# Two gate products inside a slab chunk, and a slab ahead of the transposes, in the rounds of layer 0

## The chip, the cores and the metric

The kernel runs on one core of a Trainium2 chip. The metric is the time on the device in microseconds. A core has TensorE (PE in the rows; PEld are its weight loads), VectorE (DVE), ScalarE (ACT), GpSimd (POOL) and SyncE (SP), whose queue starts all the DMA transfers here. The engines run side by side; each works through its own instructions in order and waits on semaphores for the others.

## The reference, cut to what matters

A two-layer backbone on 1024 latent tokens and 256 context tokens (1280 in all) with 1024 features. Only layer 0 is touched by the change. With h the normed and modulated input:

```python
z = h @ w_in                         # 1024 -> u, g, f, gf, 1024 columns each
u = centred_depthwise_conv(u, w_conv, b_conv)      # 4 taps
for d in range(2):                                 # both directions
    r = sigmoid(block_diag_linear(u, w_a[d], b_a[d]))
    i = sigmoid(block_diag_linear(u, w_x[d], b_x[d]))
    log_a = -8 * r * softplus(-lam[d])
    a = exp(log_a)
    b = sqrt(-expm1(2 * log_a)) * (i * u)
    y += linear_scan(a, b)                         # over tokens
f = fft2(f grouped by 128 channels, axes=(tokens, channels)).real
mix = concatenate([y * silu(g), (f @ w_f + b_f) * silu(gf)])
out = mix @ w_out
```

Matrix products are computed to nearly float32 precision: each operand is split into a high and a low part, and three products (high by high, high by low, low by high) are summed. The kernel calls such a triple mm3.

## The kernel before, in words

Layer 0 begins with a setup (norm, modulation), which makes `h_hi` and `h_lo`, eight blocks of 128 features by 1280 tokens. Then come eight rounds, t = 0 to 7, each for 128 channels. The first and the last are written out, the six between are a loop. The text counts them as rounds one to eight. A round multiplies four slabs of 128 columns of `w_in` by h, named SLAB_U, SLAB_F, SLAB_GF and SLAB_G (in the text U, F, GF, G). Tokens fall into three chunks of 512, 512 and 256 (`CHUNKS`). All the four slab products go to the same three PSUM banks `slab`, one for each chunk, so a bank must be read before the next slab writes it. The other products (gates, transposes, DFT, its second stage UV) share the PSUM buffer `W`, and `W4`.

Order of TensorE in a round before (`body`, L854): U, F (in round one both are made beside the setup, U in `slab` and F in `W`), transposes of f (L866), two small products with w_f (L874), six gate products of direction 0, GF, six gate products of direction 1, the DFT (30 products), G, and UV. A gate product k writes bank k mod 4 of `W`, and from k = 4 on it waits on `gr` for the tanh that read that bank. Product k = 6d + 3x + c belongs to direction d, gate x and chunk c.

Order of ScalarE: w_hi of F, u from PSUM, first tap of the convolution (L535), w_hi of GF, gate weights `gw_hi`, `u_hi` (L543), f from PSUM (L548), in round one the tanh of the two rows of conditions (L557), the transposed f from PSUM (L560), `ab_hi`, then for direction 0 the six tanh of the gates (L498) and three functions of the whole (L505, L507, L511), w_hi of G (L482), `y_hi` (L568, it shares the tile pq_hi), the square root (L516), tanh of GF (L574), and direction 1 in the same way; `pq_hi` (L577) comes after the DFT.

Order of VectorE: convolution taps, products with the modulation weights (`mod_sums`, L610, which use the tile E as ScalarE's L505 does), butterflies of the DFT, then for direction 0 the product i*u (L683), the term under the root (L686), b (L691), two scans (L697, L700), after these `sgf` (L711, three pieces, which read the slab banks of GF and count up `sgfd`), direction 1, `pq_lo` (L717), the scan backwards (L704), the gate of G (L721, three pieces, which count up `sg`), and the output. GpSimd makes the low parts: `w_lo` (L759), `gw_lo`, `u_lo` (L769), `y_lo` (L772). SP loads slabs of weights into `wraw` in one order for all (`body`, L430). SLAB_G's product waits for `sgfd`, SLAB_U's for `sg`.

After layer 0 come its output projection (L1183), layer 1's projections (L1453), attention and the last projection (L2016), which the change doesn't touch.

Of the kernel before, what the change touches and what calls it, by code (L numbers as in the profile page):

```python
# [23 lines left out]
ACT = mybir.ActivationFunctionType  # L24
# [3 lines left out]
KT = D // P  # L28
# [5 lines left out]
CHUNKS = [(0, 512), (512, 512), (1024, 256)]  # L34
# [311 lines left out]
def mixers(nc, a, h_hi, h_lo, work, cols, silu_c, gs, ident, mods, wraw, w_hi, w_lo, slab, W, W4, before):  # L346
    ctx = ExitStack()
    with ctx:
# [8 lines left out]
        u_hi, u_lo = sb("u_hi", [P, T], F32R), sb("u_lo", [P, T], F32R)  # L357
        cur = sb("cur", [P, ALL_COLS])
        gw = sb("gw", [P, 4, P])
        gw_hi, gw_lo = sb("gw_hi", [P, 4, P], F32R), sb("gw_lo", [P, 4, P], F32R)  # L360
        A, B, C, H, sgf, fT, xf, u = (work[:, i, :] for i in range(KT))
# [50 lines left out]
        @blk.sync  # L412
        def _(sp):
            def load_slab(t, j, first):
                if not (first and j < 2):
                    sp.wait_ge(wl[j % 2], 2 * t + j // 2)
                sp.dma_start(wraw[:, j % 2, :], a["w_in0"][4 * t + j]).then_inc(w_ld[j % 2], 16)

            def store(t):
                sp.wait_ge(mr, t + 1)  # L420
                sp.dma_start(a["mixT"][t], H[:]).then_inc(mrs, 16)
                sp.wait_ge(mf, t + 1)
                sp.dma_start(a["mixT"][t + KT], xf[:]).then_inc(mfs, 16)

            def load_mod(t, q, first):
                if not (first and q < 2):
                    sp.wait_ge(mp, 2 * (N_MOD * t + q - 1))
                sp.dma_start(wm1[:, q % 2, :], a["wm1"][t, q]).then_inc(m_ld[q % 2], 16)

            def body(t, first, last):  # L430
                if first:
                    load_mod(t, 0, True)
                    load_mod(t, 1, True)
                    sp.wait_ge(zero, 2)
                else:
                    sp.wait_ge(gwl, t)
                for c in range(2):
                    sp.dma_start(gw[HEAD * c:HEAD * (c + 1), :, HEAD * c:HEAD * (c + 1)],
                                 a["w_gate"][t, HEAD * c:HEAD * (c + 1), :, :]).then_inc(gw_ld, 16)
                if not first:  # L440
                    sp.wait_ge(abp, t)
                sp.dma_start(wf[:], a["w_f"][t]).then_inc(wf_ld, 16)
                load_slab(t, SLAB_GF, first)
                load_slab(t, SLAB_G, first)
                if not first:
                    store(t - 1)
                load_mod(t, 2, first)
                if not last:
                    load_slab(t + 1, SLAB_U, False)
                load_mod(t, 3, first)  # L450
                if not last:
                    load_slab(t + 1, SLAB_F, False)
                    load_mod(t + 1, 0, False)
                    load_mod(t + 1, 1, False)

            set_sync(sp, lambda j: load_slab(0, j, True))
            sp.wait_ge(hl, 4)
            for raw, at in tab_pieces:
                sp.dma_start(raw, a["tables"][:, at]).then_inc(tab_ld, 16)
            sp.wait_ge(modk, KT)  # L460
            sp.dma_start(silu_b[:], a["c_rows"].partition_broadcast(P)).then_inc(cb_ld, 16)
            sp.dma_start(dft_ch[:], a["dft_ch"]).then_inc(par, 16)
            loops(sp, body)
            store(KT - 1)
            sp.wait_ge(ge, 2)
            for i in range(2):
                sp.dma_start(a["gp"][i].rearrange("w (k n) -> (w k) n", n=P), g_rows[:, i, :]).then_inc(gst, 16)
            sp.wait_ge(mrs, 16 * KT)
            sp.wait_ge(mfs, 16 * KT)
            sp.wait_ge(gst, 32)  # L470
# [3 lines left out]
        def _(act):  # L474
            def split_hi(t, j, first=False):

                act.wait_ge(w_ld[j % 2], 16 * (2 * t + j // 2 + 1))
                if j >= 2:
                    act.wait_ge(done[j - 2], 3 * t + 3)
                elif not first:  # L480
                    act.wait_ge(done[j + 2], 3 * t)
                nc.scalar.activation(w_hi[:, j % 2].rearrange("p k n -> p (k n)"), wraw[:, j % 2, :],  # L482
                                     ACT.Copy).then_inc(wh[j % 2], 1)
# [30 lines left out]
            def root(t, d):  # L514
                act.wait_ge(om, 2 * t + d + 1)
                nc.scalar.activation(C[:], C[:], ACT.Sqrt).then_inc(sq, 1)  # L516

            def body(t, first, last):
                if not first:
                    split_hi(t, SLAB_F)  # L520
# [12 lines left out]
                if not first:  # L533
                    act.wait_ge(mp, 2 * N_MOD * t + 2)
                nc.scalar.activation(E[:], u_raw[:, 0:CONV_N], ACT.Identity, scale=cur[:, C_CONV:C_CONV + 1],  # L535
                                     bias=cur[:, C_BCONV:C_BCONV + 1]).then_inc(tap0, 1)
                split_hi(t, SLAB_GF)
                act.wait_ge(gw_ld, 32 * t + 32)
                if not first:
                    act.wait_ge(gp_, 12 * t)  # L540
# [2 lines left out]
                nc.scalar.activation(u_hi[:], u[:], ACT.Copy).then_inc(uh, 1)  # L543
                if not first:
                    act.wait_ge(yd, t)
                for c, (at, n) in enumerate(CHUNKS):
                    act.wait_ge(s_f, 3 * t + c + 1)
                    nc.scalar.activation(fT[:, at:at + n], (W if first else slab)[:, c, 0:n], ACT.Copy).then_inc(fr, 1)  # L548
                if not first:
                    act.wait_ge(mfs, 16 * t)  # L550
                if first:
                    act.wait_ge(cb_ld, 16)
                    act.wait_ge(conv, 2)
                    for w in range(2):
                        if w:
                            act.wait_ge(sbd, 1)
                        nc.scalar.activation(E[:, 0:D], silu_b[:, w, :], ACT.Tanh, scale=0.5).then_inc(thb, 1)  # L557
                for c, (at, n) in enumerate(CHUNKS):
                    act.wait_ge(trd, 3 * t + c + 1)
                    nc.scalar.activation(xf[:, at:at + n], W[:, c, 0:n], ACT.Copy).then_inc(xr, 1)  # L560
                act.wait_ge(abp, t + 1)
                nc.scalar.activation(ab_hi[:], W4[:, 0:256], ACT.Copy).then_inc(abh, 1)
                gates(t, 0, first)
# [220 lines left out]
        def _(pe):  # L784
            def mm3(out, l_hi, l_lo, r_hi, r_lo, start, stop):
                nc.tensor.matmul(out, l_hi, r_hi, start=start, stop=False)  # L786
                nc.tensor.matmul(out, l_hi, r_lo, start=False, stop=False)  # L787
                return nc.tensor.matmul(out, l_lo, r_hi, start=False, stop=stop)  # L788
# [9 lines left out]
                        if k == KT - 1:  # L798
                            last.then_inc(done[j], 1)

            def slab_product(t, j, first):
                pe.wait_ge(wl[j % 2], 2 * t + j // 2 + 1)
                for c, (at, n) in enumerate(CHUNKS):

                    if j == SLAB_F:
                        pe.wait_ge(ur, 3 * t + c + 1)
                    elif j == SLAB_GF:
                        pe.wait_ge(fr, 3 * t + c + 1)
                    elif j == SLAB_G:
                        pe.wait_ge(sgfd, 3 * t + c + 1)  # L810
                    elif not first:
                        pe.wait_ge(sg, 3 * (t - 1) + c + 1)
                    for k in range(KT):
                        last = mm3(slab[:, c, 0:n], w_hi[:, j % 2, k, :], w_lo[:, j % 2, k, :],
                                   h_hi[:, k, at:at + n], h_lo[:, k, at:at + n], k == 0, k == KT - 1)
                    last.then_inc(done[j], 1)

            def gate_products(t, d):
                for x in range(2):
                    for c, (at, n) in enumerate(CHUNKS):  # L820
                        k = 6 * d + 3 * x + c
                        if k < 3:
                            pe.wait_ge(xr, 3 * t + k + 1)
                        elif k > 3:
                            pe.wait_ge(gr, 12 * t + k - 3)
                        mm3(W[:, k % 4, 0:n], gw_hi[:, 2 * d + x, :], gw_lo[:, 2 * d + x, :],
                            u_hi[:, at:at + n], u_lo[:, at:at + n], True, True).then_inc(gp_, 1)

            def dft_product(t):
                pe.wait_ge(gr, 12 * t + 12)  # L830
# [23 lines left out]
            def body(t, first, last_):  # L854
                if first:
                    set_tensor(pe, first_products)
                else:
                    slab_product(t, SLAB_U, first)
                    slab_product(t, SLAB_F, first)
                pe.wait_ge(fr, 3 * t + 3)  # L860
                if first:
                    pe.wait_ge(par, 16)
# [10 lines left out]
                for x in range(2):  # L873
                    last = nc.tensor.matmul(W4[:, x * P:(x + 1) * P], dft_ch[:, x * P:(x + 1) * P], wf[:],  # L874
                                            start=True, stop=True)
                last.then_inc(abp, 1)
                pe.wait_ge(gwl, t + 1)
                pe.wait_ge(ul, t + 1)
                gate_products(t, 0)
                slab_product(t, SLAB_GF, first)  # L880
                gate_products(t, 1)
                dft_product(t)
                slab_product(t, SLAB_G, first)
                pe.wait_ge(pql, t + 1)
                pe.wait_ge(abl, t + 1)

# [1271 lines left out]
```

## Time and profile before

| | us |
|---|---|
| median of 3 runs | 1574.29 |
| lowest, highest | 1569.56, 1576.51 |
| profiled execution, span from first to last instruction | 1569.5 |
| TensorE busy (share of the span) | 1405.4 (90%) |
| VectorE busy | 856.1 (55%) |
| ScalarE busy | 729.8 (46%) |
| GpSimd busy | 572.1 (36%) |
| mean granted TensorE clock | 0.955 |

The profiled execution's time is its span, which is as long as the lowest of the runs. A busy engine's share is a mean over stages; the first 90 us are the setup, layer 0's rounds last until about 680 us, and the rest is the output projection and layer 1. TensorE's clock has two levels, 2.4 GHz (1.00 in the rows) and 1.2 GHz (0.50).

### The profile page before, as it was taken

What the parts mean: (1) busy time and instruction counts of PE and PEld (TensorE: products, weight loads), DVE (VectorE), ACT (ScalarE), POOL (GpSimd) and SP (SyncE); (2) the same over time, 40 slices, a digit from 0 to 9 for tenths busy, and PEclk for the clock granted to TensorE, in tenths of its full rate; (3) what the DMA queues carried; (4) which work ended last, traced back from release to release, by engine and by line L of the source; (5) the groups of instructions that cost most, each with busy time, mean ns of one, the idle gap of its engine ahead of it and who ended that gap; (6) DMA issues with size and microseconds to landing.
All of it is one profiled execution on the core that took longest, in us unless ns stands there. A gap on an engine that the chain in (4) does not pass through costs nothing. (4 is left out here: it accounts for less than half of the span.)

```text
span 1569.5 us, 19994 instructions
## 1 busy us (share of the span) xinstructions
PE 1405.4 (90%) x7136; PEld 1161.0 (74%) x7136; DVE 856.1 (55%) x1216; ACT 729.8 (46%) x1146; POOL 572.1 (36%) x267
## 2 busy tenths in 40 slices
PE   4968999999999999938999985999996999998697
PEld 2557888888888888836888864878885788887576
DVE  4577768677758686743111125122221888887532
ACT  3356364554656373733122213132221888887321
POOL 0013222331313323235244323434442666665432
PEclk7978999999999999969999996999998999999799
DMA  9131212122121212055433416634335533222674
GB/s 378 33 125 60 88 59 87 63 101 86 67 92 53 101 49 90 12 175 209 126 102 111 130 65 219 161 94 127 101 108 144 200 94 89 91 83 68 187 220 129
DMA packets 95284, 179.61 MB, mean 114 GB/s; under 512 B 10464, under 2 KB 57344, under 8 KB 92928
## 3 DMA queue, kind: packets, MB, share of 16 engines
q1 hardware_dynamic: 95232, 178.93, 35.4%
q8 instruction: 31, 0.51, 0.1%
q14 instruction: 21, 0.17, 0.0%
HBM read 123.84 MB, written 45.11 MB: 108 GB/s over the span
## 5 line engine op out<-in xcount | busy, mean ns | idle before, releaser
L786 PE MATMUL slab<-h_hi,w_hi 128*128 128x512 f32 x744 | 265.9, 357 | 0.1
L788 PE MATMUL slab<-h_hi,w_lo 128*128 128x512 f32 x744 | 265.3, 357 | 0.0
L787 PE MATMUL slab<-h_lo,w_hi 128*128 128x512 f32 x744 | 265.2, 356 | 0.0
L759 POOL TENSOR_TENSOR w_lo<-wraw,w_hi 128x1024 fp32r<-128x1024 f32 x32 | 81.6, 2551 | 421.6 <-ACT w_hi L482 421.6
L1738 POOL TENSOR_TENSOR probs<-probs,rdenom 128x2560 f32<-128x2560 f32 (+1 forms) x32 | 135.7, 4242 | 57.9 <-DVE rdenom L1698 57.9
L786 PEld LDWEIGHTS slab<-h_hi,w_hi 128*128 128x128 f32 x744 | 139.6, 188 | 23.2 <-DVE h_lo L259 0.3
L787 PEld LDWEIGHTS slab<-h_lo,w_hi 128*128 128x128 f32 x744 | 139.6, 188 | 22.7
L788 PEld LDWEIGHTS slab<-h_hi,w_lo 128*128 128x128 f32 x744 | 139.6, 188 | 22.7
L1453 PE MATMUL slab<-h_hi,w_hi 128*128 128x512 f32 (+1 forms) x352 | 135.5, 385 | 18.0 <-DVE h_lo L1375 18.0
L1183 PE MATMUL Y<-wo_hi,m_hi 128*128 128x512 f32 x320 | 127.6, 399 | 23.6 <-DVE wo_lo L1098 19.6
L1454 PE MATMUL slab<-h_lo,w_hi 128*128 128x512 f32 (+1 forms) x352 | 134.9, 383 | 0.0
L1455 PE MATMUL slab<-h_hi,w_lo 128*128 128x512 f32 (+1 forms) x352 | 134.6, 382 | 0.0
L1184 PE MATMUL Y<-wo_lo,m_hi 128*128 128x512 f32 x320 | 125.8, 393 | 0.0
L1185 PE MATMUL Y<-wo_hi,m_lo 128*128 128x512 f32 x320 | 125.6, 393 | 0.0
L1715 DVE TENSOR_TENSOR pt_lo<-TB,pt_hi 128x512 fp32r<-128x512 f32 x152 | 104.1, 685 | 33.7 <-ACT pt_hi L1661 32.0
L1635 ACT ACTIVATE probs<-probs,neg_max 128x640 f32<-128x640 f32 (+1 forms) x128 | 102.7, 803 | 24.9 <-DVE neg_max L1690 24.4
L1690 DVE CUSTOM_DVE_ANT_0 probs<-S,mask,nsink 128x640 f32<-128x640 f32 (+1 forms) x128 | 107.5, 842 | 1.5 <-PE S L1765 1.3
L1764 PE MATMUL S<-kd_hi,q_parts 128*128 128x256 f32 (+2 forms) x256 | 88.2, 349 | 13.9 <-DMA q_parts<-qT 12.5
L610 DVE SCALAR_TENSOR_TENSOR E<-wm,silu_bcast 128x1024 f32<-128x1024 f32 x64 | 97.6, 1525 | 5.5 <-DMA wm<-in_wm 1.1
L1661 ACT ACTIVATE pt_hi<-TB 128x512 fp32r<-128x512 f32 x152 | 89.5, 589 | 22.1 <-PE TB L1799 22.1
L1799 PE MATMUL TB<-ident,probs 128*128 128x128 f32 x608 | 91.0, 272 | 1.5 <-POOL probs L1738 1.5
L1799 PEld LDWEIGHTS TB<-ident,probs 128*128 128x128 f32 x608 | 75.6, 140 | 22.2 <-issue 1.7
(257 smaller groups left out, 3010.8 us busy)
## 6 DMA issues: line engine op xcount, KB each, us to landing
wraw<-in_w_in SPq DMA_DIRECT2D x32, 512.0 KB, 3.6
wm<-in_wm SPq DMA_DIRECT2D x32, 512.0 KB, 3.4
mixT<-work SPq DMA_DIRECT2D x16, 640.0 KB, 4.0
mraw<-mixT SPq DMA_DIRECT2D x20, 512.0 KB, 4.7
wm<-in_wm SPq DMA_DIRECT2D x8, 1024.0 KB, 20.4
q_parts<-qT SPq DMA_DIRECT2D x32, 256.0 KB, 4.6
oT<-o_out SPq DMA_DIRECT2D x8, 1024.0 KB, 3.9
work<-in_xT SPq DMA_DIRECT2D x8, 640.0 KB, 11.7
```

The source lines that it names most:

```text
L786: nc.tensor.matmul(out, l_hi, r_hi, start=start, stop=False)
L787: nc.tensor.matmul(out, l_hi, r_lo, start=False, stop=False)
L788: return nc.tensor.matmul(out, l_lo, r_hi, start=False, stop=stop)
L1183: nc.tensor.matmul(out, m_hi[:, s, h, k, :], w_hi, start=(h == 0 and k == 0), stop=False)
L1184: nc.tensor.matmul(out, m_hi[:, s, h, k, :], w_lo, start=False, stop=False)
L1185: last = nc.tensor.matmul(out, m_lo[:, s, h, k, :], w_hi, start=False, stop=(h == 1 and k == KT - 1))
L1453: nc.tensor.matmul(out, w_hi[:, j, k, :], rhs_hi, start=(k == 0), stop=False)
L1454: nc.tensor.matmul(out, w_hi[:, j, k, :], rhs_lo, start=False, stop=False)
L1455: last = nc.tensor.matmul(out, w_lo[:, j, k, :], rhs_hi, start=False, stop=(k == KT - 1))
L1690: nc.vector.tensor_tensor_reduce(out=row(b, pr[:, u, h, :]), in0=S[:, j % 2, at:768], in1=m, scale=-SCALE, scalar=nsink[:, j:j + 1], op0=A ...
L1738: nc.gpsimd.tensor_tensor(rows, rows, rden[:, u, :].unsqueeze(2).to_broadcast(rows.shape), ALU.mult).then_inc(pn, 1)
L1799: last = nc.tensor.transpose(TB[:, n_par(b, u, x), h * P:(h + 1) * P], pr[:, u, h, x * P:(x + 1) * P], ident[:])
```

## The change

On TensorE a slab product can now be issued by chunks, and a chunk by halves (`slab_chunk` with k0 and k1), and the gate products by a range.

- All rounds: gate products 4 and 5 of direction 0 stand behind the first half (k = 0 to 3, 12 products) of a GF chunk (chunk 0, in round one chunk 2). Gate products 10 and 11 stand behind the first half of G's chunk 0, and its second half comes ahead of the DFT. G's chunks 1 and 2 stay behind the DFT.
- Round one: chunk 0 of GF is issued ahead of the transposes, chunk 1 behind the products with w_f. Chunk 0 of GF waits for `ur` in place of `fr`. ScalarE copies f and the transposed f (`f_rows`, `f_tokens`) right behind w_hi of GF, ahead of gw_hi, u_hi and the condition rows. SP loads GF and G right behind the tables.

```diff
@@ SP, body and ahead of it
-                load_slab(t, SLAB_GF, first)
-                load_slab(t, SLAB_G, first)
-                if not first:
+                if not first:
+                    load_slab(t, SLAB_GF, first)
+                    load_slab(t, SLAB_G, first)
                     store(t - 1)
...
                 sp.dma_start(raw, a["tables"][:, at]).then_inc(tab_ld, 16)
+            load_slab(0, SLAB_GF, True)
+            load_slab(0, SLAB_G, True)
             sp.wait_ge(modk, KT)
@@ ScalarE
+            def f_rows(t, first):
+                for c, (at, n) in enumerate(CHUNKS):
+                    act.wait_ge(s_f, 3 * t + c + 1)
+                    nc.scalar.activation(fT[:, at:at + n], (W if first else slab)[:, c, 0:n], ACT.Copy).then_inc(fr, 1)
+
+            def f_tokens(t):
+                for c, (at, n) in enumerate(CHUNKS):
+                    act.wait_ge(trd, 3 * t + c + 1)
+                    nc.scalar.activation(xf[:, at:at + n], W[:, c, 0:n], ACT.Copy).then_inc(xr, 1)
...
                 split_hi(t, SLAB_GF)
+                if first:
+                    act.wait_ge(hl, 2 * KT)
+                    f_rows(t, first)
+                    f_tokens(t)
                 act.wait_ge(gw_ld, 32 * t + 32)
...
                 if not first:
                     act.wait_ge(yd, t)
-                for c, (at, n) in enumerate(CHUNKS):
-                    act.wait_ge(s_f, 3 * t + c + 1)
-                    nc.scalar.activation(fT[:, at:at + n], (W if first else slab)[:, c, 0:n], ACT.Copy).then_inc(fr, 1)
-                if not first:
+                    f_rows(t, first)
                     act.wait_ge(mfs, 16 * t)
+                    f_tokens(t)
...
-                for c, (at, n) in enumerate(CHUNKS):
-                    act.wait_ge(trd, 3 * t + c + 1)
-                    nc.scalar.activation(xf[:, at:at + n], W[:, c, 0:n], ACT.Copy).then_inc(xr, 1)
                 act.wait_ge(abp, t + 1)
@@ TensorE
+            def slab_chunk(t, j, c, first, k0=0, k1=KT):
+                at, n = CHUNKS[c]
+                if k0 == 0:
+                    if c == 0:
+                        pe.wait_ge(wl[j % 2], 2 * t + j // 2 + 1)
                     if j == SLAB_F:
                         pe.wait_ge(ur, 3 * t + c + 1)
                     elif j == SLAB_GF:
-                        pe.wait_ge(fr, 3 * t + c + 1)
+                        pe.wait_ge(ur if first else fr, 3 * t + c + 1)
                     elif j == SLAB_G:
                         pe.wait_ge(sgfd, 3 * t + c + 1)
...
+                for k in range(k0, k1):
+                    last = mm3(slab[:, c, 0:n], w_hi[:, j % 2, k, :], w_lo[:, j % 2, k, :],
+                               h_hi[:, k, at:at + n], h_lo[:, k, at:at + n], k == 0, k == KT - 1)
+                if k1 == KT:
                     last.then_inc(done[j], 1)
...
+                if first:
+                    slab_chunk(t, SLAB_GF, 0, first)
                 pe.wait_ge(fr, 3 * t + 3)
...
                 last.then_inc(abp, 1)
+                if first:
+                    slab_chunk(t, SLAB_GF, 1, first)
                 pe.wait_ge(gwl, t + 1)
                 pe.wait_ge(ul, t + 1)
-                gate_products(t, 0)
-                slab_product(t, SLAB_GF, first)
-                gate_products(t, 1)
+                gate_products(t, 0, range(0, 4))
+                slab_chunk(t, SLAB_GF, 2 if first else 0, first, 0, 4)
+                gate_products(t, 0, range(4, 6))
+                slab_chunk(t, SLAB_GF, 2 if first else 0, first, 4, KT)
+                if not first:
+                    slab_chunk(t, SLAB_GF, 1, first)
+                    slab_chunk(t, SLAB_GF, 2, first)
+                gate_products(t, 1, range(0, 4))
+                slab_chunk(t, SLAB_G, 0, first, 0, 4)
+                gate_products(t, 1, range(4, 6))
+                slab_chunk(t, SLAB_G, 0, first, 4, KT)
                 dft_product(t)
-                slab_product(t, SLAB_G, first)
+                slab_chunk(t, SLAB_G, 1, first)
+                slab_chunk(t, SLAB_G, 2, first)
```

## Rows read from the trace of the kernel before

**Rows 1.** The page: its span, and GpSimd's low part of a slab.

```profile
span 1569.5 us, 19994 instructions
...
L759 POOL TENSOR_TENSOR w_lo<-wraw,w_hi 128x1024 fp32r<-128x1024 f32 x32 | 81.6, 2551 | 421.6 <-ACT w_hi L482 421.6
```

**Rows 2.** One period (A:B, length, busy by engine, PEclk), and TensorE's wait in it.

```profile
234.20:307.40 73.20, 71.36 (x382) 60.46 (x381) 53.08 (x63) 40.99 (x50) 21.38 (x8) 1.00 0.23 78
...
PE W L786 <- ACT work L498: 1.4, 2, 1.1
```

**Rows 3.** TensorE in order of time (start, length), round two.

```profile
191.12 0.48 PE L786 MATMUL W<-u_hi,gw_hi 128*128 128x512 f32 x1
...
194.72 0.39 PE L786 MATMUL slab<-h_hi,w_hi 128*128 128x512 f32 x1
...
208.72 0.39 PE L786 MATMUL W<-u_hi,gw_hi 128*128 128x512 f32 x1
...
214.04 0.39 PE L786 MATMUL W<-tab_hi,pq_hi 128*128 128x256 f32 x1 [1.15 <-ACT work L498]
...
217.67 0.39 PE L786 MATMUL slab<-h_hi,w_hi 128*128 128x512 f32 x1
...
234.14 0.40 PE L786 MATMUL slab<-h_hi,w_hi 128*128 128x512 f32 x1
```

**Rows 4.** ScalarE and VectorE in order of time, round two, and a window of it.

```profile
192.10 3.52 ACT L498 ACTIVATE work<-W,cur 128x512 f32<-128x512 f32 x6
...
195.50:204.50 9.00, 9.00 (x40) 7.23 (x39) 5.25 (x13) 8.93 (x8) 3.68 (x2) 1.00 0.01 4
...
204.53 2.99 DVE L691 SCALAR_TENSOR_TENSOR work<-work 128x1280 f32<-128x1280 f32 x1 [3.70 <-ACT work L516]
...
210.64 1.59 DVE L711 SCALAR_TENSOR_TENSOR work<-work,slab 128x512 f32<-128x512 f32 x3
...
218.07 1.65 ACT L577 ACTIVATE pq_hi<-W 128x1792 fp32r<-128x1792 f32 x1
...
228.38 0.69 DVE L721 SCALAR_TENSOR_TENSOR work<-work,slab 128x512 f32<-128x512 f32 x1 [0.67 <-ACT work L584]
```

**Rows 5.** Round one: order of time on three engines, and a window.

```profile
92.52 1.46 ACT L535 ACTIVATE E<-u_raw,cur 128x1282 f32<-128x1282 f32 x1
...
97.00:103.50 6.50, 0.00 (x0) 0.00 (x0) 3.91 (x3) 4.09 (x6) 5.05 (x3) 0.50 0.08 31
...
103.52 1.28 ACT L557 ACT_TABLE_LOAD   x1
...
103.55 0.48 PE L866 MATMUL W<-ident,work 128*128 128x128 f32 x1 [11.15 <-ACT work L548]
...
118.30 1.46 ACT L505 ACTIVATE E<-work,cur 128x1280 f32<-128x1280 f32 x1 [3.42 <-DVE E L610]
...
135.41 1.59 DVE L711 SCALAR_TENSOR_TENSOR work<-work,slab 128x512 f32<-128x512 f32 x3
```

**Rows 6.** Four waits of TensorE after layer 0, each with the window behind it.

```profile
713.16 0.77 PE L1183 MATMUL Y<-wo_hi,m_hi 128*128 128x512 f32 x1 [2.28 <-POOL wo_lo L1151]
...
713.10:716.50 3.40, 3.34 (x8) 2.69 (x9) 2.13 (x2) 1.16 (x2) 2.12 (x1) 0.51 0.69 228
...
724.84 0.50 PE L1183 MATMUL Y<-wo_hi,m_hi 128*128 128x512 f32 x1 [3.06 <-DVE wo_lo L1098]
...
724.80:728.20 3.40, 2.53 (x10) 1.79 (x11) 2.08 (x1) 2.96 (x4) 3.32 (x2) 1.00 0.99 388
...
969.18 0.77 PE L1453 MATMUL slab<-h_hi,w_hi 128*128 128x512 f32 x1 [3.21 <-DVE h_lo L1375]
...
969.10:972.40 3.30, 3.21 (x8) 2.58 (x9) 3.24 (x1) 0.39 (x1) 2.16 (x1) 0.50 0.00 0
...
1479.55 0.50 PE L2016 MATMUL Y<-wo_hi,m_hi 128*128 128x512 f32 x1 [2.43 <-POOL m_lo L1983]
...
1481.00:1484.40 3.40, 3.40 (x9) 2.67 (x9) 3.37 (x3) 0.00 (x0) 2.74 (x1) 0.50 0.00 0
```

More of the change, by code:

```diff
@@ L799, in first_products @@
                             last.then_inc(done[j], 1)
-            def slab_product(t, j, first):
-                pe.wait_ge(wl[j % 2], 2 * t + j // 2 + 1)
-                for c, (at, n) in enumerate(CHUNKS):
+            def slab_chunk(t, j, c, first, k0=0, k1=KT):
[3 more added lines that the diff above has]
+                        pe.wait_ge(wl[j % 2], 2 * t + j // 2 + 1)
                     if j == SLAB_F:
@@ L812, in slab_product, with gate_products @@
                         pe.wait_ge(sg, 3 * (t - 1) + c + 1)
-                    for k in range(KT):
-                        last = mm3(slab[:, c, 0:n], w_hi[:, j % 2, k, :], w_lo[:, j % 2, k, :],
-                                   h_hi[:, k, at:at + n], h_lo[:, k, at:at + n], k == 0, k == KT - 1)
+                for k in range(k0, k1):
+                    last = mm3(slab[:, c, 0:n], w_hi[:, j % 2, k, :], w_lo[:, j % 2, k, :],
+                               h_hi[:, k, at:at + n], h_lo[:, k, at:at + n], k == 0, k == KT - 1)
+                if k1 == KT:
                     last.then_inc(done[j], 1)
[L818 to L827, printed above, removed]
+            def slab_product(t, j, first):
+                for c in range(3):
+                    slab_chunk(t, j, c, first)
+            def gate_products(t, d, ks):
+                for k in ks:
+                    x, c = k // 3, k % 3
+                    at, n = CHUNKS[c]
+                    k += 6 * d
+                    if k < 3:
+                        pe.wait_ge(xr, 3 * t + k + 1)
+                    elif k > 3:
+                        pe.wait_ge(gr, 12 * t + k - 3)
+                    mm3(W[:, k % 4, 0:n], gw_hi[:, 2 * d + x, :], gw_lo[:, 2 * d + x, :],
+                        u_hi[:, at:at + n], u_lo[:, at:at + n], True, True).then_inc(gp_, 1)
             def dft_product(t):
```

## The prediction

> **What bounds the kernel now.** I read the share of busy time first, then the waits of TensorE, and then one round in order of time. The profiled execution spans 1569.5 us, and the three timed runs go from 1569.56 to 1576.51, so next to nothing lies around the span; the sum below is made against 1569.5, and carried over to the median of 1574.29, which is 4.8 above it [rows 1]. Rounds two to eight of layer 0 repeat to a hundredth of a microsecond with a period of 73.2 us. TensorE is busy for 71.4 of it at full clock, and waits 1.4 us for ScalarE's tanh of the gate products [rows 2]. So a round is bound by TensorE, but a second chain runs just beside it: gate products of direction 0, tanh (L498), three exponentials, two splits, root, b-term, scan. ScalarE has no gap in the middle of that chain (8.9 busy of 9.0 us) [rows 4]. VectorE begins to empty the first slab bank (L711) at 210.64, while TensorE gets through its four free gate products of direction 1 at 211.2 (208.72 plus 3.5 units of 0.70) [rows 3, 4]. The two chains meet within half a microsecond, and what makes the second longer will soon be seen.
>
> Durations: from 194.72 to 208.72 one slab of 48 products of 512 columns and 24 of 256 takes 14.00 us, so 0.233 us per 512 columns, 2.80 for half a chunk, 5.60 for a chunk, 0.70 or 0.35 for a gate product [rows 3].
>
> **Rounds two to eight, step by step.**
> 1. Direction 0. Gate products 0 to 3 take 2.45 us from 191.12, as before. Then 2.80 us of slab GF go ahead of products 4 and 5. Before, ScalarE's six tanh ended at 195.62 (192.10 plus 3.52) [rows 3, 4]. Product 4 now starts at 196.46 and product 5 ends its turn at 197.51; with the lag of 0.9 us that the rows show from there to the end of the sixth tanh (194.72 to 195.62), it ends near 198.4: 2.78 later. ScalarE works in order and without a gap behind it, so exponentials, w_hi of slab G, y_hi and root move by 2.78. TensorE gains nothing here, since it had no wait at products 4 and 5: the 18 products took 3.60 of the ideal 3.50 [rows 3]. The cover that was given away is that of ScalarE's chain.
> 2. The b-term is 2.99 us long at 204.53, because GpSimd's y_lo runs into it; y_lo comes from the same ScalarE chain and moves with it, so this keeps its length. The Trainium skill ("SBUF — State Buffer", "The single rule") calls this an exclusive lock between the two engines, which agrees with that row. L711's three pieces (512, 512, 256 columns in 1.59 us) begin at 213.42 and the first ends at 214.1 [rows 4].
> 3. The new first half of slab G's chunk 0 writes the bank that this piece reads: it waits for sgfd. TensorE is through with products 6 to 9 at 211.2 and waits until 214.2, about 3 us. Queued behind the waiting product are the last two gate products, the rest of chunk 0, the DFT. Before, TensorE came to slab G only after the DFT, and sgfd was long there.
> 4. From 214.2: 2.80 of slab, 1.05 of gate products 10 and 11, 2.80 of slab, so the DFT starts at 220.85 instead of 214.04. The wait for the last tanh is really gone: their tanh end near 218.9, by the same lag of 0.9.
> 5. From the DFT's start two ways lead to the next round. TensorE: before, 20.10 us to 234.14; now one chunk less, 14.50: 235.35. The other: DFT 3.63, then pq_hi (218.07 before, 0.4 behind the DFT, of which the exponentials made 0.2), and 11.00 us from there to the end of the first L721 piece (228.38 plus 0.69), whose read frees the bank for the next slab U. I take 3.63 + 0.2 + 11.0 + 0.1 = 14.95: 235.8 [rows 3, 4]. The later one counts: **+1.67 us per round**, for six rounds 10.0. The eighth has no next slab U and splits one slab less; there the TensorE way counts, +1.2.
>
> One term hangs on how fast the products follow each other. The trace has 233 ns for 512 columns [rows 3]. The Trainium skill ("TensorE: Matmul & The Clock Gate", "Wait — 56ns, not 53.3ns?") gives N over 2.4 GHz plus some 2.5 ns, 216 ns for 512 columns. By the Trainium skill's figure the three half chunks that are new on the path would be 0.6 us shorter, and the round +1.0 instead of +1.67. The row is of these very products, so the sum keeps it.
>
> **Clock.** A stall of 3 us is new. The trace has four of about that length: after those of 2.28, 2.43 and 3.21 us a stretch of 3.4 us follows at 0.5 of the clock (1.2 GHz), after one of 3.06 us none [rows 6]. In such a stretch eight 512-column products run in 3.4 us instead of fourteen and a half: 1.55 us lost, all of it on the path. Three in four over seven rounds: **+8.1**, bounds 0 and 10.9; twice the upper one if the clock needs two such stretches to come back.
>
> **Round one.** Loads of slabs GF and G go behind the tables, where SP's queue is idle; they are the same two DMAs, moved ahead of silu rows, channel DFT, two wm1 pieces, gate weights and W_f, all of which wait for modk, so that they are issued no later than before. ScalarE is done with the first tap at 93.98 and makes w_hi, some 1 us, without waiting for a transfer, GpSimd w_lo takes 2.55, and chunk 0 of GF starts at 97.6 instead of the transposes at 103.55 [rows 1, 5]. With some 4 us of it at half clock it ends near 105.2, so the transposes come 1.7 later than before. ScalarE waits for them in front of gw_hi and u_hi. Of its 4.1 us of work in 97.0 to 103.5 (w_hi, gw_hi, u_hi, three copies of equal size to those of the transposes) all but w_hi's 1 us now follows the first transposed bank (106.0, an estimate: 0.8 behind the first transpose), so its next piece, the table load for the tanh of the condition rows, moves from 103.52 to 109.3: +5.8. Behind that table load stand silu rows, VectorE's six mod_sums, and the exponential at 118.30, which waited 3.4 us for exactly these [rows 5]. So the whole chain moves by 5.8, and L711's first piece ends at 135.41 + 0.69 + 5.8 = 141.9. Chunk GF0 fills half of TensorE's 11.15 us gap, but the work done early only makes TensorE wait at G's chunk 0: the transposes, W_f and GF1 last to 112.5, the gate products of direction 0 with GF2 to 119.0, four more gate products to 121.5, and there TensorE stands until 142. Then 10.3 us to the DFT's end, plus 2.0 for half clock: 154.4; plus 0.2 + 11.0 + 0.1: slab U at 165.8, against 160.94 before (234.14 less a period). **+4.9**; the bounds I take are 3 and 7 (no half clock at all, or twice as long).
>
> Sum: 4.9 + 10.0 + 1.2 + 8.1 = **24.2 us**. The profiled execution becomes 1593.7, the median 1598.5. Behind layer 0 nothing changes.
>
> **Rivals.** 0.5% of this kernel, about what a measurement can tell from no change, is 7.9 us.
> - *No half clock.* As above, but the stall doesn't bring the clock down. For it: one of four stalls didn't; against it: the three that did. 16.1 us, 1590.4.
> - *Long half clock.* Each stall is followed by two stretches at 0.5: 7 times 3.1 in place of 8.1, +38, 1612. For it: round one's gap of 11 us kept the clock at 0.5 to its end [rows 5]; against it: after three shorter stalls it was 3.4 us each time [rows 6].
> - *Round one gives its gap back.* If the mod_sums chain weren't put off by the transposes, the 11.15 us of idle would be won, and the rounds' loss of 19 remains: +8, 1582. Against it: ScalarE's order of instructions.
> - *The other side: ScalarE's chain has slack.* The point is the delay of the last tanh. At 2.78 us a round gets 1.67 longer; it is one for one, so below 1.1 us of delay the round gets shorter. With none, TensorE reaches slab G at 211.4, the next U comes at 233.0, -1.1 a round, and round one -1.2: -9, 1565. Against it: 8.9 busy of 9.0 us on ScalarE [rows 4].
>
> **Numbers.** Forecast 0.56; no half clock 0.20; long half clock 0.07; round one gives back 0.07, half of it below +7.9; other side 0.06, small mixtures near nothing 0.04. So faster by over 0.5% 0.06, within 0.5% 0.08, slower 0.86. The range goes from 1584, which leaves out the last two cases and part of the third rival, to 1610. Predicted: 1598.5.
>
> **What the changed profile would show.** Per round TensorE waits some 3 us at the first slab product behind gate product 9, released by VectorE L711's line, and none at the DFT; period near 76; half-clock stretches near most of those waits. In round one no long wait before the transposes, but one of about 20 us before slab G. It would be wrong if the period stayed under 73.2: then the sixth tanh wasn't on the chain; or if ScalarE's table load in round one came before 106.

## The result, and the profile after

The changed kernel takes 1596.37 us (median of 4 runs, 1593.73 to 1601.22), the kernel before 1573.67 in the same comparison (1569.56 to 1576.51). The ratio is 1.0157, with a 95% interval of 1.0135 to 1.0178: some 25 us slower (21 to 28); the two medians themselves lie 22.7 apart. The profiled execution spans 1596.2 us, within a timed execution of 1597.96.

Both traces hold a mark that the setup and layer 1 don't touch: from ScalarE's first copy of u out of PSUM (91.12 before, 92.40 after) to the last products of layer 0, the two transposes of `mods` (679.7 before). Between them lie the eight rounds and nothing else. Below, "in layer 0" means this stretch, in the one profiled execution of a kernel: 588.6 us before. It has a spread of its own, in round one: in the traces of seven kernels here whose round one has the same instructions, the kernel before among them, slab U of round two starts between 68.6 and 70.7 us behind the first copy of u. So of a difference in layer 0, up to 2 us can be chance; the six periods behind repeat to 0.2 us where the clock is full.

The page of the changed kernel, its head and its group of slab products (line 797 is the first product of mm3, line 722 is L711 of before, line 732 is L721):

```profile
span 1596.2 us, 19995 instructions
...
L797 PE MATMUL slab<-h_hi,w_hi 128*128 128x512 f32 x744 | 272.7, 367 | 48.4 <-DVE work L722 40.8
```

The two transposes at the end of layer 0 in the view of instructions by tile (least, median and most ns of one, then the start of the first and of the last):

```profile
L929 PE MATMUL W<-ident,mods x2: 380/398/417, 706.1 to 706.3; 128*16 128x128 f32 x2
```

706.1 less 92.40 is 613.7 us in layer 0: +25.1. The slab products, which waited for nothing before, now wait 40.8 us for VectorE's reading of the slab banks. The waits for the tanh [rows 2] are gone from the list, and so is the one of 11 us ahead of round one's transposes [rows 5]:

The waits of TensorE in the whole of the changed kernel (sum, count, longest):

```profile
PE slab L797 <- DVE work L722: 40.8, 8, 20.7
...
PE slab L797 <- POOL w_lo L770: 5.4, 1, 5.4
...
PE W L886 <- ACT work L523: 3.3, 7, 0.5
PE slab L797 <- DVE work L732: 2.1, 7, 0.4
```

Round four of the changed kernel, which ran at full clock, in order of time on TensorE: slab U, slab G's chunk 0, the DFT, the rest of slab G, the next slab U. It answers to [rows 3].

```profile
321.11 0.50 PE L797 MATMUL slab<-h_hi,w_hi 128*128 128x512 f32 x1 [0.30 <-DVE work L732]
...
374.50 0.47 PE L797 MATMUL slab<-h_hi,w_hi 128*128 128x512 f32 x1 [2.88 <-DVE work L722]
...
381.22 0.28 PE L797 MATMUL W<-tab_hi,pq_hi 128*128 128x256 f32 x1
...
384.73 0.40 PE L797 MATMUL slab<-h_hi,w_hi 128*128 128x512 f32 x1
...
396.01 0.50 PE L797 MATMUL slab<-h_hi,w_hi 128*128 128x512 f32 x1 [0.30 <-DVE work L732]
```

The same round as a window: its length, the busy time of TensorE, its weight loads, VectorE, ScalarE and GpSimd, the granted clock, the DMA share and GB/s:

```profile
321.11:396.01 74.90, 71.25 (x380) 60.26 (x380) 53.18 (x64) 40.80 (x51) 21.35 (x9) 1.00 0.22 76
```

The period is 74.90 where it was 73.20. From slab U to the DFT (the product at 381.22) it is 60.11 us (53.10 before), and from the DFT to the next slab U 14.79 (20.10 before).

ScalarE at the same place of round two, to be held beside [rows 4]: four tanh, a gap for the half chunk, the last two, and the exponential.

```profile
198.26 2.45 ACT L500 ACTIVATE work<-W,cur 128x512 f32<-128x512 f32 x4
203.52 1.05 ACT L500 ACTIVATE work<-W,cur 128x512 f32<-128x512 f32 x2 [2.81 <-PE W L799]
204.47 1.46 ACT L507 ACTIVATE E<-work,cur 128x1280 f32<-128x1280 f32 x1
```

The 7 us behind each of the seven waits of 2.8 to 2.9 us; the last column but two is the granted clock:

```profile
220.40:227.40 7.00, 7.00 (x20) 5.57 (x21) 0.77 (x2) 2.06 (x5) 0.00 (x0) 0.57 0.02 4
298.00:305.00 7.00, 6.96 (x25) 5.63 (x26) 1.37 (x3) 3.27 (x7) 0.00 (x0) 0.76 0.00 0
374.50:381.50 7.00, 7.00 (x33) 5.77 (x34) 2.27 (x3) 4.84 (x8) 0.00 (x0) 1.00 0.00 0
449.40:456.40 7.00, 7.00 (x33) 5.77 (x34) 2.25 (x3) 4.82 (x8) 0.00 (x0) 1.00 0.00 0
524.30:531.30 7.00, 7.00 (x20) 5.61 (x21) 0.76 (x2) 2.11 (x5) 0.00 (x0) 0.57 0.00 0
601.90:608.90 7.00, 7.00 (x25) 5.67 (x26) 1.37 (x3) 3.27 (x7) 0.00 (x0) 0.76 0.00 0
678.30:685.30 7.00, 7.00 (x33) 5.77 (x34) 2.24 (x3) 4.75 (x7) 0.00 (x0) 1.00 0.01 2
```

Four waits have low clock (1.2 GHz) behind them, two for nearly all of the 7 us and two for about half; three have none. The reader sees it in the number of products: 20, 25 or 33 in the same time. Slab U starts at 167.03, 244.68, 321.11, 396.01, 470.90, 548.53 and 625.04, so the six periods are 77.65, 76.43, 74.90, 74.89, 77.63 and 76.51. Twice 74.9 stands where the clock was full, some 2.7 more where it was low for long, some 1.6 more where for half of that.

Round one of the changed kernel, beside [rows 5]:

```profile
99.09 0.79 PE L797 MATMUL slab<-h_hi,w_hi 128*128 128x512 f32 x1 [5.42 <-POOL w_lo L770]
...
110.53 1.28 ACT L571 ACT_TABLE_LOAD   x1
...
125.86 1.45 ACT L507 ACTIVATE E<-work,cur 128x1280 f32<-128x1280 f32 x1 [6.05 <-DVE E L621]
...
143.63 0.76 PE L797 MATMUL slab<-h_hi,w_hi 128*128 128x512 f32 x1 [20.70 <-DVE work L722]
...
167.03 0.50 PE L797 MATMUL slab<-h_hi,w_hi 128*128 128x512 f32 x1 [0.20 <-DVE work L732]
```

This trace reached ScalarE's first copy of u 1.28 us later than that of before, so from each of these times 1.28 is taken: the table load stands at 109.25 (103.52 before), the exponential at 124.58 (118.30), slab U of round two at 165.75 (160.94).

So the +25.1 us in layer 0 are: round one +4.8; six periods, 458.0 against 439.0 (before they are 73.12 to 73.20 us each), +19.0; the last round and what follows it +1.3. Of the 19.0, 10.4 is the longer period at full clock (six times 74.90 less 439.0), and 8.6 the low clock. This split is that of one execution; in the others the low clock may have had another share, since the mean clock was 0.953 in the quickest of the four and 0.947 in the slowest.

### The profile page after: what moved, and what is told of

It is laid out like the page before. It is cut to its first block and busy times, and to the rows that moved or that the text cites. A ratio compares the mean times of both kernels' runs of the same rounds, so it can differ in the third digit from the quotient of the medians.

```text
span 1596.2 us, 19995 instructions
## 1 busy us (share of the span) xinstructions
PE 1415.2 (89%) x7136; PEld 1167.6 (73%) x7136; DVE 855.3 (54%) x1216; ACT 727.7 (46%) x1146; POOL 571.6 (36%) x267
## 5 line engine op out<-in xcount | busy, mean ns | idle before, releaser
L797 PE MATMUL slab<-h_hi,w_hi 128*128 128x512 f32 x744 | 272.7, 367 | 48.4 <-DVE work L722 40.8
L798 PE MATMUL slab<-h_lo,w_hi 128*128 128x512 f32 x744 | 269.8, 363 | 0.0
L799 PE MATMUL slab<-h_hi,w_lo 128*128 128x512 f32 x744 | 269.4, 362 | 0.0
L798 PEld LDWEIGHTS slab<-h_lo,w_hi 128*128 128x128 f32 x744 | 142.8, 192 | 22.7
L1484 PE MATMUL slab<-h_hi,w_hi 128*128 128x512 f32 (+1 forms) x352 | 135.4, 385 | 18.7 <-DVE h_lo L1406 18.1
## 6 DMA issues: line engine op xcount, KB each, us to landing
work<-in_xT SPq DMA_DIRECT2D x8, 640.0 KB, 12.4
```

Of the source, the lines that this page charges most:

```text
L1484: nc.tensor.matmul(out, w_hi[:, j, k, :], rhs_hi, start=(k == 0), stop=False)
```

## The experiments

Theory: two chains run side by side; the split in direction 0 makes ScalarE's longer, slab G's chunk 0 meets the bank that VectorE reads only behind the scan, and the low clock comes on top; in round one the place of ScalarE's copy puts off the condition rows. The rivals are in the expectations. Each kernel was timed beside the kernel before. The ratio stands with its 95% interval, and beside it the change in layer 0, which is free of what varies outside that layer.

**One part alone.** Round one only; direction 0 only; direction 1 only (the last two with round one as before):

```diff
 # round one only: rounds two to eight as before
-                gate_products(t, 0, range(0, 4))
...
+                gate_products(t, 0, range(0, 6))
+                slab_chunk(t, SLAB_GF, 0, first, 0, KT)
...
+                gate_products(t, 1, range(0, 6))
+                dft_product(t)
+                slab_chunk(t, SLAB_G, 0, first, 0, KT)
...
 # direction 0 only
                 gate_products(t, 0, range(0, 4))
                 slab_chunk(t, SLAB_GF, 0, first, 0, 4)
                 gate_products(t, 0, range(4, 6))
...
+                gate_products(t, 1, range(0, 6))
+                dft_product(t)
+                slab_chunk(t, SLAB_G, 0, first, 0, KT)
...
 # direction 1 only
+                gate_products(t, 0, range(0, 6))
+                slab_chunk(t, SLAB_GF, 0, first, 0, KT)
...
                 gate_products(t, 1, range(0, 4))
                 slab_chunk(t, SLAB_G, 0, first, 0, 4)
                 gate_products(t, 1, range(4, 6))
                 slab_chunk(t, SLAB_G, 0, first, 4, KT)
                 dft_product(t)
```

> Only round one is changed (slab GF ahead of the transposes, the new order of ScalarE and SP, its own gate products and slab G as in the changed kernel); rounds two to eight are those of before. Theory (ScalarE's wait for the transposes puts off the condition rows, the mod_sums and with them the scan): +4.9 us, TensorE waits some 20 us at slab G of round one, and the period stays 73.2. Rival (the 11 us gap ahead of the transposes is won): -8 to -11 us. Rival (round one has no part in it): 0.

Measured: ratio 1.0041 (1.0026 to 1.0056), +6 us; in layer 0 +6.2. TensorE's wait at slab G of round one is 20.67 us, and the periods behind stay at 73.16 to 73.24. The gap of 11 us that the slab fills is not won, and round one is worse for it.

> Only gate products 4 and 5 of direction 0 stand behind half of GF's chunk 0, in rounds two to eight; direction 1, slab G and round one are as before. Theory (the last tanh of direction 0 is at the head of the chain to the scan, and its delay goes through one for one): the scan ends 2.8 us later, TensorE waits 3 us for the tanh of gate product 6, the period at full clock is 76.0 (+2.8), and half-clock stretches come on top: +19.5 and some 8, so +24 to +30 us. Rival (ScalarE's chain has slack): 0 to +3 us.

Measured: ratio 1.0243 (1.0229 to 1.0257), +38 us; in layer 0 +37.0. The direction is the theory's, the amount is above its range. In the trace the wait is the forecast one. It stands at gate product 10, since the tanh of direction 1 that has to free its bank starts only behind the scan. What was wrong is the clock:

```profile
215.82 0.50 PE L792 MATMUL W<-u_hi,gw_hi 128*128 128x512 f32 x1 [3.00 <-ACT work L498]
218.28 0.58 PE L792 MATMUL W<-tab_hi,pq_hi 128*128 128x256 f32 x1 [0.69 <-ACT work L498]
```

The first line is the wait ahead of gate product 10, the second the one behind it, ahead of the transform. The windows behind three of the seven waits:

```profile
215.80:222.80 7.00, 6.29 (x27) 5.80 (x28) 3.82 (x5) 6.57 (x8) 0.00 (x0) 0.55 0.01 4
294.00:301.00 7.00, 6.03 (x27) 5.60 (x28) 3.82 (x5) 6.58 (x8) 0.00 (x0) 0.57 0.00 0
...
450.80:457.80 7.00, 5.86 (x27) 5.51 (x28) 3.83 (x5) 6.50 (x8) 0.00 (x0) 0.58 0.00 0
```

All seven waits have a clock between 0.55 and 0.61 in the 7 us behind them, where I had counted on three in four at half the length.

> Only direction 1: gate products 10 and 11 stand inside slab G's chunk 0, which comes ahead of the DFT, in rounds two to eight; direction 0 and round one are as before. Theory: the bank is free at 211.4 when TensorE comes at 211.2, so the wait at slab G is 0.2 us instead of 2.9, the DFT starts 4.1 later but the two waits of 1.4 us are filled, the period is 72.1 (-1.1, set by the chain behind the DFT), no half clock in rounds two to eight: -8 us. Rival (slab G ahead of the DFT is itself what costs, since pq, root and the second scan start later): +1 to +4 us a round, +7 to +28.

Measured: ratio 0.9952 (0.9938 to 0.9966), -8 us; in layer 0 -7.7. The period is 72.1 (slab U at 233.41, 305.51 and 377.61), no wait stands ahead of slab G, and 0.30 us at slab U. So direction 1's part gains 8 us alone, and slab G ahead of the DFT costs nothing by itself. Direction 0's part costs 37 alone, and it turns the whole into a loss.

**The clock alone.** The time in which TensorE would wait is filled with products that nobody reads, in the changed kernel and in the one with direction 0 alone (there ahead of gate product 10).

```diff
                 gate_products(t, 1, range(0, 4))
+                if not first:
+                    pe.wait_ge(abl, t + 1)
+                    for i in range(24):
+                        nc.tensor.matmul(W4[:, 256:512], u_hi[:, 0:P], h_hi[:, 0, 0:256], start=True, stop=True)
                 slab_chunk(t, SLAB_G, 0, first, 0, 4)
```

> The changed kernel, and in rounds two to eight TensorE makes 24 products of 256 columns, whose result nobody reads, in the time in which it would wait for slab G's bank (2.8 of 2.9 us). Theory (the stall's half clock costs some 8 us of the change's 23, and the rest is the longer chain): all rounds at 1.00 of the clock, period 74.9 everywhere, +15 to +17 us against before. Rival (the clock has no part, the work is late for another reason): as the changed kernel, +23 us, or more for the added products.

Measured: ratio 1.0108 (1.0091 to 1.0126), +17 us; in layer 0 +16.8 against +25.1 of the changed kernel. The period is 74.87 to 74.97, also in the rounds where the clock had been low, and from 150 to 660 us all is at 1.00:

```profile
168.06:242.93 74.87, 74.10 (x405) 63.25 (x405) 53.20 (x64) 40.81 (x51) 21.36 (x9) 1.00 0.23 77
```

24 more products in each of rounds two to eight, and the kernel is 8 us faster. The low clock is 8.3 us of the change's 25.

> The kernel with the split in direction 0 alone, with 24 products of 256 columns (2.8 us) that nobody reads ahead of gate product 10 in rounds two to eight. Theory (its +37 us are 7 times 2.8 for the chain and 7 times 2.5 for half clock): the clock stays at 1.00, the period is 76.0, +19 to +21 us against before. Rival (the chain got longer by more than the split): 78 us a round, +34 to +38.

Measured: ratio 1.0139 (1.0124 to 1.0155), +22 us; in layer 0 +20.3, with the clock at 1.00 from 200 to 660 us. That settles the miss above: of 37.0 us, 20.3 are the longer chain and 16.7 (2.4 a round) the clock.

**How much delay a round bears.** Direction 1 with halves, round one as before, and the amount of GF ahead of gate products 4 and 5 varied (it is 0 in "direction 1 only", and 4 in the changed kernel).

```diff
-                slab_chunk(t, SLAB_GF, 0, first, 0, 4)
+                slab_chunk(t, SLAB_GF, 0, first, 0, 2)      # or 0, KT
                 gate_products(t, 0, range(4, 6))
-                slab_chunk(t, SLAB_GF, 0, first, 4, KT)
+                slab_chunk(t, SLAB_GF, 0, first, 2, KT)     # or nothing
```

> Round one as before. In rounds two to eight direction 1 as in the changed kernel; in direction 0 a quarter of GF's chunk 0 (k = 0 and 1, 1.4 us) stands ahead of gate products 4 and 5 instead of a half (2.8 us). Theory (one for one through ScalarE's chain, from the 72.1 us period that no delay gives): the delay of the scan is 1.4, TensorE waits 1.5 us at slab G's chunk 0, the period is 73.5, so +2 us; half-clock stretches unlikely after a wait of 1.5. Rival (the split costs by its being there, not by its length): a period near 74.9 plus half clock, +12 to +19 us.

Measured: ratio 1.0009 (0.9998 to 1.002), +1 us; in layer 0 +1.0. The six periods are 2.1 us longer than before in sum, as the theory has it; round one, whose instructions are those of before, came out 0.9 shorter. The clock is 1.00 behind all seven waits.

> As the last one, with the whole chunk 0 of GF (5.6 us) ahead of gate products 4 and 5. Theory: delay 5.6, TensorE waits 5.7 us at slab G's chunk 0, the period at full clock is 77.7, and every round has some 6.8 us at half clock (2.5 us lost), so 80 us a round and +45 to +50 us. Rival (a threshold: once ScalarE is late, later makes no difference): as the changed kernel, +19 to +24 us.

Measured: ratio 1.0275 (1.0258 to 1.0291), +43 us; in layer 0 +46.3. The timed runs' +43 is a little below the expected 45 to 50, the trace within it. All seven waits have a low clock behind them, 0.57 to 0.78 in 7 us. The waits of the two at slab G's chunk 0 are 1.50 and 5.67 us, and the periods:

| GF ahead of products 4, 5 | wait at slab G | period at full clock |
|---|---|---|
| 0 | none | 72.1 |
| 1.4 us | 1.46 to 1.50 | 73.5 |
| 2.8 us (the change) | 2.88 | 74.9 |
| 5.6 us | 5.67 | not seen; 79.0 to 80.3 with low clock |

One for one, as far as full-clock rounds show it: the period is 72.1 plus the delay. By these rows the break-even with 73.2 is at 1.1 us of delay.

**The bank alone.** The changed kernel, with VectorE's first sgf piece ahead of the two scans:

```diff
                     if d == 0:
+                        gate_gf(0)            # L711's piece for chunk 0
...
                         nc.vector.tensor_tensor_scan(H[:, N_LAT:T], ...)
-                for c, (at, n) in enumerate(CHUNKS):
-                    gate_gf(c)
+                gate_gf(1)
+                gate_gf(2)
```

> The changed kernel, but VectorE empties slab bank 0 of GF (first piece of sgf) ahead of the two scans instead of behind them, in all rounds. Direction 0 keeps its delay of 2.8 us. Theory (what hurts is that slab G's chunk 0 waits for a bank that is read only behind the scan): the bank is free at the time TensorE comes, the wait at slab G vanishes, one of 0.9 us stands at gate product 10, the period is 72.9, no half clock in rounds two to eight, and the whole is +0 to +4 us against before, 20 less than the changed kernel. Rival (the late scan itself is what costs): a period of 74.9 or more, +20 us.

Measured: ratio 0.9988 (0.9978 to 0.9998); in layer 0 +0.1. The ratio's -2 us is a little better than the expected 0 to +4. All of the wait for slab G in rounds two to eight is gone, 0.66 us stands at gate product 10, and the clock is 1.00 from 200 to 660 us. The period is 72.8. With this one line moved the change costs nothing in all: round one is still 2.8 us longer, and the rounds behind win that back. So in rounds two to eight the changed kernel pays for the bank's late reading, and for the low clock behind that wait. The late scan by itself costs 0.7 us a round here (72.8 against 72.1), which is the wait at product 10: the half chunk of slab G, 2.8 us that now run without waiting, covers the rest of the late tanh. Where nothing covers it, in direction 0 alone with the fillers, the period is 75.9, all of the 2.8 us.

**Quarters.** What these point to: leave direction 0 whole and put two quarters of slab G's chunk 0 around products 10 and 11.

```diff
+                gate_products(t, 0, range(0, 6))
...
                 gate_products(t, 1, range(0, 4))
+                slab_chunk(t, SLAB_G, 0, first, 0, 2)
                 gate_products(t, 1, range(4, 6))
+                slab_chunk(t, SLAB_G, 0, first, 2, 4)
                 dft_product(t)
+                slab_chunk(t, SLAB_G, 0, first, 4, KT)
```

> Round one and direction 0 as before; in rounds two to eight of direction 1 a quarter of slab G's chunk 0 (k = 0 and 1, 1.4 us) goes ahead of gate products 10 and 11 and a quarter behind them, the rest behind the DFT. Theory: both waits of before (0.2 and 1.15 us) are filled, the DFT starts 1.2 us later than before and not 4.1, so that TensorE and not the chain behind the DFT sets the period: 71.6 (-1.6), -11 us against before, 3 better than direction 1 with halves. Rival (quarters are too short to cover the tanh, so the waits come back at the DFT): a period of 72.1 to 72.6, -4 to -8 us.

Measured: ratio 0.9911 (0.9896 to 0.9927), -14 us, where -11 was expected; in layer 0 -12.2, the period 71.6. Of the 12.2, 11.0 lie in rounds two to eight, as forecast, against 7.7 with halves; 1.2 are round one, whose instructions are those of before. TensorE's waits from 200 to 660 us come down to the one ahead of the transposes:

```profile
PE W L879 <- ACT work L521: 2.8, 6, 0.5
```

And one period of it as a window:

```profile
200.00:271.60 71.60, 71.02 (x382) 60.35 (x381) 52.98 (x64) 41.15 (x51) 21.37 (x8) 1.00 0.24 80
```

**Round one again**, on top of quarters. First the copy of the transposed f back in its old place; then, with chunk 1 of GF behind the gate products, VectorE's mod_sums 1 and 2 behind the sgf pieces.

```diff
 # both: ScalarE, round one
                     f_rows(t, first)
-                    f_tokens(t)
...
                         nc.scalar.activation(E[:, 0:D], silu_b[:, w, :], ACT.Tanh, scale=0.5).then_inc(thb, 1)
+                    f_tokens(t)
 # the second only: VectorE, round one, and the waits of ScalarE for mp
-                mod_sums(t, 1)
-                mod_sums(t, 2)
...
+                mod_sums(t, 1)
+                mod_sums(t, 2)
                 direction(1)
```

> Rounds two to eight as the kernel with quarters (period 71.6). Round one takes over from the changed kernel that slab GF is loaded early and its chunks 0 and 1 stand around the transposes, but ScalarE copies the transposed f where it did before, behind gw_hi, u_hi and the tanh of the condition rows; direction 0 unsplit, direction 1 with quarters. Theory (the copy's place on ScalarE is what put off the mod_sums chain, by 5.8 us; without it the chain stands where it was or 1.3 us earlier): -12 to -16 us against before, that is up to 2 better than quarters alone and 6 better than with the changed kernel's round one. TensorE still waits some 20 us for the scan. Rival (GF ahead of the transposes is what costs): -8 us or less of gain.

Measured: ratio 0.9936 (0.9922 to 0.9949), -10 us, which is short of the expected -12 to -16; in layer 0 -13.0, within it. The runs don't tell it from quarters alone, and neither does layer 0: the 0.8 us between them is less than what round one varies by. The trace does tell that the changed kernel's round one costs by the place of the copy:

```profile
104.74 1.28 ACT L570 ACT_TABLE_LOAD   x1
...
119.95 1.46 ACT L507 ACTIVATE E<-work,cur 128x1280 f32<-128x1280 f32 x1 [1.15 <-DVE E L621]
```

The first copy of u is at 92.81 in this trace, so the table load comes 11.9 us behind it and the exponential 27.1. In the kernel before it is 12.4 and 27.2, in the changed kernel 18.1 and 33.5. Here too chunk 0 of GF stands ahead of the transposes, and they come 14.4 us behind the mark as in the changed kernel (12.4 before); so it is not the slab that puts off the condition rows. TensorE's wait ahead of slab G is 14.40 us and not 20.7, shorter by as much as the exponential comes earlier. The 11 us gap ahead of the transposes is not won in either: it has moved to slab G.

> Rounds two to eight with quarters. Round one: GF loaded early, its chunk 0 ahead of the transposes, chunks 1 and 2 behind direction 0's gate products; the copy of the transposed f behind the tanh of the condition rows; and VectorE makes four of the six mod_sums of that stage behind the sgf pieces instead of ahead of the butterflies. Theory (round one is bound by the mod_sums ahead of the exponential at 118.3): scan and slab U of round two come 6 to 8 us earlier, -18 to -22 us against before. Rival (the mod_sums behind the scan put off direction 1 by as much): -12 to -14 us, as quarters alone.

Measured: ratio 0.9882 (0.9867 to 0.9897), 1553.17 us against 1572.39, -19 us; in layer 0 -19.2. The exponential of direction 0 starts without a wait at 114.86, in the trace whose first copy of u is at 92.72, so 22.1 us behind it where it was 27.1; TensorE's wait ahead of slab G is down to 6.69:

```profile
111.52 3.46 ACT L500 ACTIVATE work<-W,cur 128x512 f32<-128x512 f32 x6
114.86 1.46 ACT L509 ACTIVATE E<-work,cur 128x1280 f32<-128x1280 f32 x1
```

Its mark at the end of layer 0, to be held beside the 706.1 of the changed kernel:

```profile
L944 PE MATMUL W<-ident,mods x2: 383/402/421, 662.1 to 662.3; 128*16 128x128 f32 x2
```

This is the fastest of all the kernels here, below both the kernel before and the changed one. Chunk 1 of GF moved together with the mod_sums, and no run separates the two.

## Why the prediction was right

The forecast was +24.2 us and 1598.5; measured are +25.1 in layer 0 and 1596.4. The mechanism was right step by step; two of the sizes came out as well as they did by chance, the clock and the last tenths of round one. By its own steps:

- *Step 1, the delay of 2.78 us on ScalarE.* Right: in round two the sixth tanh ends at 204.57 (203.52 plus 1.05). Round two starts 6.09 later than before, so it is 2.86 later than it was. The dose shows it too: 1.4, 2.8 and 5.6 us ahead give waits of 1.5, 2.9 and 5.7.
- *Steps 2 and 3, the bank and the wait of 3 us.* Right: 2.88. That the bank is the place is shown by the kernel that reads it ahead of the scans.
- *Step 4, the DFT.* Forecast 6.81 later within the round, measured 7.01 (60.11 against 53.10).
- *Step 5, +1.67 a round by the chain behind the DFT.* Right: 74.90 less 73.20 is 1.70, and slab U is released by VectorE's sg piece, with 0.2 to 0.4 us of wait, in every round. The last round: forecast +1.2, measured +1.3.
- *Clock, +8.1.* The sum is right (8.6 in the profile, 8.3 by the filler), its making was not: three in four waits at 1.55 us each were counted; four of seven came, two at some 1.6 and two at some 2.7, so that the rivals "no half clock" and "long half clock" each had a part of it. The kernel with direction 0 alone shows how much luck was in it: there seven of seven came at about 2.4, and my expectation of 24 to 30 us was passed by 7 to 8.
- *Round one, +4.9.* Right: table load +5.7 (forecast +5.8), slab U +4.8. Shown by two runs: that part alone costs 4 to 9 us, and with the copy in its old place table load and exponential stand where they stood before. That slab U agrees to 0.1 is chance: the same round one gave +6.0 in the trace of that part alone and +5.0 in that with the fillers.
- *The other side.* It asked for slack in ScalarE's chain. There is none, but there was 1.1 us between the period without delay (72.1) and that of before, as it said.
- Two things were said wrongly without a consequence. One is that next to nothing lies around the span: the changed kernel's profiled execution has 1.8 us beside it, and later executions of the kernel before have as much (1573.82 against a span of 1572.0). The other is that the rounds before repeat to a hundredth of a microsecond: their periods go from 73.12 to 73.20.

## What to carry to other kernels

Before moving products of the bound engine into a gap, ask who consumes what they are moved in front of: here the gap was on TensorE and the slack wasn't, since the tanh behind two moved products headed a chain on ScalarE that had no idle time in it. A shared PSUM buffer turns "earlier" into a wait on its last reader, and that reader's place in another engine's order may be the thing to move. And fill a wait in portions of about its length: around waits of 0.2 and 1.15 us, quarters of 1.4 us gained 11.0 us in rounds two to eight, where halves of 2.8 us gained 7.7.

## What the runs showed of the hardware that I had not expected

- Waits of nearly the same length differed in what the clock did behind them. With direction 0 alone the wait was 3.00 us in rounds two to seven and 2.83 in the eighth, and each time the 7 us behind it were granted 0.55 to 0.61; with the changed kernel's 2.88 us, three of seven had 1.00. The waits of the first kernel ended 78.2 to 78.5 us apart, where the chain alone, with the fillers, gives 75.9. Why the two differ stays open: behind the 3.00 us a second wait of 0.7 to 1.1 us follows, which the changed kernel hasn't, and no run here has the one without the other. Waits of 1.5 us (a quarter ahead of products 4 and 5) never brought the clock down in seven rounds, waits of 5.7 us did in seven of seven.
- The Trainium skill ("TensorE: Matmul & The Clock Gate", "The HAM clock gate") says that the default is the low clock and that activity releases it. The fillers fit that: with the waits filled the clock stayed at 1.00, and 24 useless products in each of rounds two to eight made the changed kernel 8 us faster, and the one with direction 0 alone 17 us.
- TensorE's products of 512 columns followed each other at 0.233 us at full clock in every kernel here, so a slab takes 14.0 us. The Trainium skill ("TensorE: Matmul & The Clock Gate", "Wait — 56ns, not 53.3ns?") puts 2.5 ns on top of columns by 2.4 GHz and gives 0.216 us for 512 columns; the measured 0.233 decides.
